# Modulation products moved into the branch tails of the first block, with the layer loop written out and one weight queue

## What is computed

```
def ada_mod(cvec, w, b):                       # w: 1024 x 6144, per layer
    return jnp.split(jax.nn.silu(cvec) @ w + b, 6, axis=-1)
...
x = first_block(...)
return second_block(x, c_2, ctx_2, c_ctx_2, ada_w_2, ada_b_2, ...)
...
# in second_block, for each of 2 layers:
sh1, sc1, g1, sh2, sc2, g2 = [... for m in ada_mod(c, ada_w[i], ada_b[i])]
csh1, csc1, cg1, csh2, csc2, cg2 = ada_mod(c_ctx, ada_w[i], ada_b[i])
...
# in first_block, the end of branch n:
sigmoid(merge[:, :, n]) * ((o * silu(gates[:, :, n])) @ w_branch[l, n])
```

## Time and profile before

| | |
|---|---|
| median of 3 runs | 5255.11 us (5243.96 to 5256.96) |
| the profiled execution | 5240.5 us, its span 5238.4 us |
| PE (TensorE matmuls) busy | 4346.1 us, 83% |
| PE weight loads busy | 3690.2 us, 70% |
| DVE (VectorE) busy | 1823.1 us, 35% |
| ACT (ScalarE) busy | 1476.7 us, 28% |
| POOL (GpSimd) busy | 1377.6 us, 26% |
| mean granted TensorE clock | 0.887 |

### The profile page before, as it was taken

How to read it: one execution, slowest core, us unless ns; L and a number is a source line. 1 busy time by engine, 2 the same in 40 slices (tenths; PEclk the granted TensorE clock), 3 DMA queues, 4 the chain that set the end, 5 groups by cost and what they waited for, 6 DMA issues and landing times. The chain is left out here.

```text
span 5238.4 us, 60561 instructions
## 1 busy us (share of the span) xinstructions
PE 4346.1 (83%) x24260; PEld 3690.2 (70%) x24260; DVE 1823.1 (35%) x3628; ACT 1476.7 (28%) x2338; POOL 1377.6 (26%) x468
## 2 busy tenths in 40 slices
PE   5798978788688988778687959999998888857888
PEld 4677867677576876767435958888887878746776
DVE  2724352423462434324002036311112655553111
ACT  2234232222233333223101136321112443432211
POOL 1121313223213222232000222122222545432333
PEclk7798989889779989889897979999998888778999
DMA  2111212211212122232363211122212011101232
GB/s 68 42 50 33 85 35 85 83 57 57 60 35 70 53 61 61 63 92 71 97 220 110 65 51 20 33 57 60 58 55 58 27 34 33 37 17 49 74 87 73
DMA packets 512868, 323.86 MB, mean 62 GB/s; under 512 B 60239, under 2 KB 508871, under 8 KB 512583
## 3 DMA queue, kind: packets, MB, share of 16 engines
q1 hardware_dynamic: 512582, 319.91, 21.2%
HBM read 316.13 MB, written 2.16 MB: 61 GB/s over the span
## 5 line engine op out<-in xcount | busy, mean ns | idle before, releaser
L70 POOL TENSOR_TENSOR w_lo<-w_raw,w_hi 128x2048 fp32r<-128x2048 f32 (+5 forms) x284 | 1126.5, 3967 | 3464.2 <-ACT w_hi L190 3464.2
L190 ACT ACTIVATE w_hi<-w_raw 128x2048 fp32r<-128x2048 f32 (+5 forms) x284 | 473.6, 1667 | 1724.3 <-PE psum L232 1683.4
L230 PE MATMUL psum<-xF_hi,w_hi 128*128 128x512 f32 x1232 | 488.4, 396 | 61.0 <-PEq L107 58.4
L231 PE MATMUL psum<-xF_lo,w_hi 128*128 128x512 f32 x1232 | 484.7, 393 | 0.0
L232 PE MATMUL psum<-xF_hi,w_lo 128*128 128x512 f32 x1232 | 484.2, 393 | 0.0
L230 PE MATMUL psum<-ffn_h_hi,w_hi 128*128 128x512 f32 (+1 forms) x1056 | 381.2, 361 | 43.5 <-POOL w_lo L70 21.3
L232 PE MATMUL psum<-ffn_h_hi,w_lo 128*128 128x512 f32 (+1 forms) x1056 | 377.9, 358 | 0.0
L231 PE MATMUL psum<-ffn_h_lo,w_hi 128*128 128x512 f32 (+1 forms) x1056 | 376.6, 357 | 0.0
L230 PE MATMUL psum<-w_hi,xF_hi 128*128 128x256 f32 (+2 forms) x960 | 283.3, 295 | 40.9 <-PEq L107 30.2
L230 PEld LDWEIGHTS psum<-xF_hi,w_hi 128*128 128x128 f32 x1232 | 234.8, 191 | 114.4 <-issue 61.7
L231 PE MATMUL psum<-w_lo,xF_hi 128*128 128x256 f32 (+2 forms) x960 | 282.4, 294 | 0.0
(11 more groups left out here) (502 smaller groups left out, 9216.2 us busy)
## 6 DMA issues: line engine op xcount, KB each, us to landing
w_raw<-in_w_in_dram SPq DMA_DIRECT2D x54, 1024.0 KB, 5.3
w_raw<-in_ada_w_dram SPq DMA_DIRECT2D x48, 1024.0 KB, 5.2
w_raw<-in_ffn_w_in_dram SPq DMA_DIRECT2D x88, 512.0 KB, 5.1
w_raw<-in_w_in_dram SPq DMA_DIRECT2D x82, 512.0 KB, 4.1
w_raw<-in_ffn_w_out_dram SPq DMA_DIRECT2D x32, 704.0 KB, 4.6
w_raw<-in_w_branch_dram SPq DMA_DIRECT2D x80, 256.0 KB, 4.3
w_raw<-in_hg_w_in_dram SPq DMA_DIRECT2D x40, 512.0 KB, 4.0
w_raw<-in_na_w_qkv_dram SPq DMA_DIRECT2D x12, 1024.0 KB, 5.1
```

Of the source, the lines that this page charges most:

```text
L70: return eng.tensor_tensor(pair.lo, src, pair.hi.bitcast(F32), ALU.subtract)
L190: act.activation(self.w(j).hi, self.raw_w(j), ACT.Copy).then_inc(self.high_done, 1)
L230: pe.matmul(out, left.hi, right.hi, start=first, stop=False)
L231: pe.matmul(out, left.hi, right.lo, start=False, stop=False)
```

## The change

1. `ada_w` leaves the weight queue. In each branch tail ScalarE issues the DMA of one 1 MB block of it into a single buffer of its own; TensorE multiplies it after merge step 1 to 5, with the eight chunks spread over four groups of 32 columns (PSUM partitions 0, 32, 64, 96), 32 stationary columns each of which two are not zero. ScalarE copies all 128 partitions out, and after the next merge step two float32 matmuls against a constant 0/1 matrix `fours` add the four groups and turn the result. VectorE adds the bias. Four tails of a layer take 5 blocks, the last one 4: 24 blocks for each of 2 layers.
2. Merge steps go round three pairs of banks, since banks 6 and 7 are taken.
3. The small columns and the sigmoid (`conditioning`) go to the start of the kernel, before the rotation tables. There the 18 gathers stand before the weight loads.
4. The loop over layers is written out, with one weight queue for the whole kernel; `layer_params` runs once, for both layers, with 12 DMAs. Flushes at the loop's end and before the second block are gone; `room` flushes where many semaphores are in use.

```diff
+    def room(self, n):
+        if len(self.spent) + n > 110:
+            self.flush(keep=(self.mm, self.high_done, self.low_done, *self.landed))
...
-def branch_tail(C, n, o, mixed):
+def branch_tail(C, w, l, n, o, mixed, mod):
...
+    blocks = range(5 * n, min(5 * n + 5, 24))
+    NM = len(blocks)
...
+                def modulate(i):
+                    if i == 0:
+                        pe.wait_ge(gated, 4)
+                    else:
+                        pe.wait_ge(ada_copied, i)
+                    pe.wait_ge(ada_in, 16 * (i + 1))
+                    for k in range(KD):
+                        r = slice(32 * (k % 4), 32 * (k % 4) + 32)
+                        last = pe.matmul(C.bank(6)[r, 0:256], mod.cc[:, k, :], ada_w[:, k, :], start=(k < 4), stop=(k >= 4))
+                    last.then_inc(ada_product, 1)
+
+                def turn_modulation(i):
+                    pe.wait_ge(ada_copied, i + 1)
+                    if i:
+                        pe.wait_ge(ada_added, i)
+                    for b in range(2):
+                        last = pe.matmul(C.bank(7)[:, 2 * b:2 * b + 2], ada_rows[:, i % 2, P * b:P * b + P], C.fours,
+                                         start=True, stop=True)
+                    last.then_inc(ada_turned, 1)
+
                 for fb in range(8):
-                    A, B = C.bank(2 * (fb % 4)), C.bank(2 * (fb % 4) + 1)
+                    A, B = C.bank(2 * (fb % 3)), C.bank(2 * (fb % 3) + 1)
...
-                    elif fb < 4:
-                        pe.wait_ge(gated, 2 * (fb - 2) + 2)
+                    elif fb == 2:
+                        pe.wait_ge(gated, 2)
                     else:
-                        pe.wait_ge(mixed_done, fb - 3)
+                        pe.wait_ge(mixed_done, fb - 2)
...
+                    if 1 <= fb <= NM:
+                        modulate(fb - 1)
+                    if 2 <= fb <= NM + 1:
+                        turn_modulation(fb - 2)
...
             @block.scalar
             def _(act):
+                def load_modulation(i):
+                    if i:
+                        act.wait_ge(ada_product, i)
+                    act.dma_start(ada_w[:, :, :], cols(w["ada_w_2"], l, 256 * blocks[i], 256)).then_inc(ada_in, 16)
+
+                load_modulation(0)
                 C.high_parts(act, base)
...
+                    if 1 <= fb <= NM:
+                        i = fb - 1
+                        act.wait_ge(ada_product, i + 1)
+                        if i + 1 < NM:
+                            load_modulation(i + 1)
+                        if i >= 2:
+                            act.wait_ge(ada_turned, i - 1)
+                        act.activation(ada_rows[:, i % 2, :], C.bank(6)[:, 0:256],
+                                       ACT.Copy).then_inc(ada_copied, 1)
...
+                    if 3 <= fb <= NM + 2:
+                        i = fb - 3
+                        dve.wait_ge(ada_turned, i + 1)
+                        at = C.bank(7)[:, 0:4].rearrange("p (b c) -> p b c", c=2)
+                        b = 2 * blocks[i]
+                        dve.tensor_tensor(mod.ada[:, l, b:b + 2, :], at, mod.bias[:, l, b:b + 2].unsqueeze(2).broadcast_to([P, 2, 2]),
+                                          ALU.add).then_inc(ada_added, 1)
...
-        C.flush()
...
-        with nc.Fori(0, 2) as l:
-            C.begin(first_layer_jobs(w, l))
-            layer_params(C, l, w)
+        layer_params(C, w, par, neg_lam, sub_gain)
+        for l in range(2):
...
-            C.flush()
...
-    jobs = []
-    for l in range(2):
-        jobs += in_pieces(of("ada_w_2", l, True), 0, 6 * D)
-    jobs += in_pieces(of("na_w_qkv_2", 0), 0, 3 * D) + in_pieces(of("na_w_o_2", 0), 0, D) + ffn_jobs(0)
+    jobs = in_pieces(of("na_w_qkv_2", 0), 0, 3 * D) + in_pieces(of("na_w_o_2", 0), 0, D) + ffn_jobs(0)
...
+            @block.sync
+            def _(sp):
+                for dst, src in loads:
+                    column_gather(sp, dst, src, columns_in)
+                C.start_weights(sp)
+                sp.wait_ge(columns_in, 16 * len(loads))
...
+def modulation_scales(C, mod, small):
...
+    with C.stage("chain") as (block, chain):
+        C.weights(block)
...
+        small = small_columns(C, ctx)
+        early = ctx.enter_context(ExitStack())
+        mod = Modulation(C, ctx, early)
+        C.begin(first_layer_jobs(w, 0) + first_layer_jobs(w, 1) + second_jobs(w))
+        conditioning(C, w, mod, small)
+        first_block(C, w, lat, hF[:, :, SEQ:768], mod)
```

More of the change, by code:

```diff
@@ L886, in branch_tail @@
         gg = ctx.enter_context(C.nc.sbuf_tensor(f"gg_{C.serial}", [P, 2, SEQ], F32))
-        with C.stage("turned", "o_ready", "gate_sig", "gated", "high", "low", "merge_sig", "mixed_done", "chain") as (
-                block, turned, o_ready, gate_sig, gated, high, low, merge_sig, mixed_done, chain):
+        with C.stage("turned", "o_ready", "gate_sig", "gated", "high", "low", "merge_sig", "mixed_done", "chain",
+                     "ada_in", "ada_product", "ada_copied", "ada_turned", "ada_added") as (
+                block, turned, o_ready, gate_sig, gated, high, low, merge_sig, mixed_done, chain,
+                ada_in, ada_product, ada_copied, ada_turned, ada_added):
             C.weights(block)
@@ L1672, in second_jobs, with __init__, sb, conditioning @@
     return jobs + in_pieces(of("hg_w_o_2", 0), 0, D) + ffn_jobs(1)
-def modulation(C, w, ada, small):
+class Modulation:
+    def __init__(self, C, ctx, early):
+        def sb(n, shape, ctx=early):
+            return ctx.enter_context(C.nc.sbuf_tensor(n, shape, F32))
+        self.ada = sb("ada", [P, 2, 48, 2], ctx)
+        self.cc = sb("cc", [P, KD, 32])
+        self.bias = sb("ada_bias", [P, 2, 48])
+def conditioning(C, w, mod, small):
     nc = C.nc
@@ L1694, in modulation @@
                      (small["hg_norm"], w["hg_norm_g_2"].rearrange("a p -> p a"))]
-            loads += [(bias[:, l, :], w["ada_b_2"][l:l + 1].rearrange("a (k p) -> p (a k)", p=P)) for l in range(2)]
+            loads += [(mod.bias[:, l, :], w["ada_b_2"][l:l + 1].rearrange("a (k p) -> p (a k)", p=P)) for l in range(2)]
             for name in ("norm1_g_2", "norm2_g_2"):
@@ L1705, in _ @@
                 C.low_parts(pool)
-            @block.sync
-            def _(sp):
-                C.start_weights(sp)
-                for dst, src in loads:
-                    column_gather(sp, dst, src, columns_in)
-                sp.wait_ge(columns_in, 16 * len(loads))
             @block.scalar
@@ L1779, in modulation, with _ @@
-        with C.stage("chain") as (block, chain):
-            @block.vector
-            def _(dve):
-                step = Chain(dve, chain)
-                for l in range(2):
-                    for q, name in ((1, "norm1_g_2"), (4, "norm2_g_2")):
-                        sc = ada[:, l, 8 * q:8 * q + 8, :]
-                        step(dve.scalar_tensor_tensor(sc, sc, 1.0, small[name][:, l, :].unsqueeze(2).broadcast_to([P, KD, 2]),
-                                                      ALU.add, ALU.mult))
+def modulation_scales(C, mod, small):
+    with C.stage("chain") as (block, chain):
+        C.weights(block)
+        @block.scalar
+        def _(act):
+            C.high_parts(act)
+        @block.vector
+        def _(dve):
+            step = Chain(dve, chain)
+            for l in range(2):
+                for q, name in ((1, "norm1_g_2"), (4, "norm2_g_2")):
+                    sc = mod.ada[:, l, 8 * q:8 * q + 8, :]
+                    step(dve.scalar_tensor_tensor(sc, sc, 1.0, small[name][:, l, :].unsqueeze(2).broadcast_to([P, KD, 2]),
+                                                  ALU.add, ALU.mult))
@@ L2490, in consts_table @@
     t["columns"] = np.concatenate(variants, 1)
+    t["fours"] = np.stack([p % 32 == c for c in range(2)], 1).astype(np.float64)
     t["inv_freq"] = np.broadcast_to(inv, (P, 24))
```

178 lines of the change are left out of this document (78 added, 100 removed).

## The result

The changed kernel is slower: 5359.62 us in the median (5345.36 to 5364.31) against 5249.53 (5240.03 to 5256.96) for the kernel before beside it, a ratio of 1.0208 (in brackets, here and below, its 95% interval: [1.0188, 1.0228]). The forecast was 5065 us. The head of the second block and the gap between the layers are gone but for a few us, as forecast; some 300 us came in that the sum did not have. The profiled execution took 5355.97 us, its span is 5354.0.

The account below looks back on a forecast made before the run. TensorE was taken to bound layers and tails; the second block's head and the layer gap were exposed. Terms -269 + 31 - 8 - 24 + 79 + 5 = -186 from 5240.5 gave 5054.5; with run spread, forecast 5065 us, range 5035 to 5180.

Parts of the forecast that it names:

- step 5: Waits and queues of the branch tails: ScalarE's wait and VectorE's addition cost nothing; late loads add 5 us (0 to 20).
- The prediction's own sign of being wrong: Wrong if the branch tails grow by more than 100 us or the start by more than 45.
- The second claim that failed: Stages from 2812 us on: the same instructions in both kernels, so no term in the sum.
- Step 1: Head of the second block, 274.3 us: all but 1.6 us and a 3.3 us later end goes, 269 us removed.
- Step 2: Conditioning at the kernel's start: gathers 14.5 us, then weights and low parts 16.5 us, 31 us added (26 to 41).
- Step 3: `layer_params` run once: 8 us removed in layer 1 (12.7 us left), 24 us in the gap before layer 2.
- Step 4: 48 modulation blocks in the tails: product 1.2 us and turn 0.44 us each, 79 us added (62 to 187).
- the figure for three tiles: Trainium skill's 2.38x for three column tiles: eight matmuls in a tail cost at least 1.45 us, sum 12 us higher.
- The rival of groups that take turns: Column groups in the tails do not overlap: 8 matmuls cost 3.46 us, 108 us more, 5173 us; chance 0.11.
- That of an emptying array: In the tails, each change between wide and narrow matmuls loses 0.163 us: 16 us, 5081 us; chance 0.12.
- Late loads: Modulation blocks landing late in a few places in the tails: 5 us added (0 to 20).
- The rival that made the kernel slower: Blocks land so late that 38 waits in the tails reach 4.9 us or more; at 6.2 us, 5300 us; chance 0.03.

Follow-up runs that it names:

- the first experiment: The changed kernel with VectorE's bias addition of a block put ahead of its wait for the merge step: 5087.94 us, ratio 0.9694.
- the change with 14 columns: The changed kernel with 14 unused columns added to the constants, nothing else changed: 5335.79 us, ratio 1.0185.

## Why the prediction was wrong, and where it was right

**The step that failed is step 5, its sentence on VectorE: "one operation on 4 columns for a block, beside 3.6 busy of 8.3 us; nothing".** It looked at how much VectorE had to do, not at what stood ahead of the addition in its queue, nor at who waited for it. For ScalarE's new wait the same step did name what was queued behind. For VectorE the question had to be asked the other way round: TensorE waits for `ada_added`, and the operation that raises it stands behind a merge-sum that depends on the TensorE step just finished. The price was in the rows of before. From the end of a merge step to the end of the sigmoid 544.70 to 546.67, 1.97 us; VectorE's merge-sum 3.58; the addition and the hand-over some 0.3, an estimate; less the 1.2 that the forecast gave to the product, which runs meanwhile: 4.65 us, 38 times 177. The trace of after says 4.83 in most steps and 179.3 in all. The rest, 87 us, is the lower clock, for which the earlier trace rows had a sign too: the gap between the layers, without TensorE, stood at 0.52. The prediction's own sign of being wrong, tails that grow by more than 100 us, came: 78 for the blocks and 268 for the waits.

**The second claim that failed** is that from 2812 us on both kernels do the same in the same time. The instructions are the same, the addresses of their activations are not. Putting these back on multiples of 64 bytes took 42 us of span off the first experiment and 25 off the change, over both blocks; of the 32 us by which the second block had grown, 24 and 21.5 went. The prediction looked for the price of each added operation and never asked what an added tensor moves.

**The other terms.**
- Step 1, head of the second block: 269 us forecast, 274.3 - 4.4 = 270 measured. Right, GpSimd's last low part included (4.50 us).
- Step 2, the conditioning: 31 forecast, 56.77 - 19.82 = 37 measured. The gathers took 18.7 us to issue, not 14.5 (the two bias rows 4.67 where 4 had been taken, four of `norm_g` 5.52 where 0.65 each had been), and VectorE's chain ended last, behind the sigmoids, not GpSimd:

```profile
19.82 0.37 SPq L1706 DMA_DIRECT2D c_in<-in_c_dram  x1
...
22.50 4.67 SPq L1706 DMA_DIRECT2D ada_bias<-in_ada_b_dram  x2
27.22 5.52 SPq L1706 DMA_DIRECT2D columns<-in_norm_g_dram  x4
...
38.55 16.77 SPq L168 DMA_DIRECT2D w_raw<-in_w_in_dram  x4
...
45.97 8.95 POOL L70 TENSOR_TENSOR w_lo<-w_raw,w_hi 128x2048 fp32r<-128x2048 f32 x2 [45.53 <-ACT w_hi L195]
...
56.12 0.17 DVE L1808 TENSOR_SCALAR columns<-columns 128x16 f32<-128x16 f32 x1
56.77 0.37 SPq L1054 DMA_DIRECT2D pos_i<-in_positions_dram  x1
```

- Step 3: `layer_params` from 105.17 to 117.75, 12.6 us (12.7 forecast); the gap between the layers 3.1 us where 28.6 were, 25 removed (24 forecast).
- Step 4: the product 9.60 - 8.42 = 1.18 us a step (1.2 forecast), the turn 0.45 (0.44). The 1.45 us that the prediction called the least by the figure for three tiles was no lower bound for four. The rival of groups that take turns is out by the run with one group. That of an emptying array is not: 1.18 is the 0.86 of four rounds and 0.32 more, just its price of 2 x 0.163, and with one group the step shows 12.17 - 8.42 = 3.75, 0.29 over the 3.46 forecast for one group. The forecast had this cost inside its 1.2 us as "some for the change"; the rival put it on top a second time.
- Late loads: 5 us forecast, none. The block lands in the time of the earlier trace rows, on the other queue too:

```profile
ada_w<-in_ada_w_dram ACTq DMA_DIRECT2D x48, 1024.0 KB, 5.2
```

- The rival that made the kernel slower had the right form, 38 waits of 4.9 us in the tails, and the wrong cause: a late block. Its chance of 0.03 was the chance of that cause alone.

**Together**, in spans: 5052 forecast (5054.5 less 2.1 outside the span), + 266 for the wait and its clock, + 42 for the operands' places, + 6 for the conditioning, - 7 for late loads and the borders = 5359, against 5354.0. The 266 and the 42 are differences between runs, so the test of the forecast is the kernel without them: its sum is 5051, its profile has 5045.7. Some of that closeness is luck, for the second block of that kernel is still 8 us longer than before, so the rest is some 13 us shorter than the sum. The structure of the forecast stood; one wait and one side effect were missing.

## What to carry to other kernels

For each semaphore that the bottleneck engine waits on, find the instruction that raises it and read what stands ahead of it in its own queue; if anything there depends on what the bottleneck has just finished, the wait is a full round trip each time, however small the operation. Count a wait on TensorE with the slower matmuls behind it, here half as much again (87 us on 179). And when a kernel gains or loses a small tensor, compare the steps of untouched stages too: they may have moved.

## What the hardware showed that was not expected

- Float32 matmuls in four groups of 32 columns run fully side by side: 8 of them in 1.07 us against 3.64 in one group. The Trainium skill ("TensorEngine Tiling (Array Packing)", "Key Properties") says that a change of tiling mode drains TensorE. The steps here agree with it: some 0.3 us beyond the columns' own time for the two changes of each block, with four groups and with one, 15 us for the 48 blocks. No run takes the change of mode alone away, so this is the likeliest reading, not shown.
- In the change the clock was at 1.2 GHz after each 4.83 us of waiting, and the rest of the step took 2.2 to 3.0 us longer. After 1.99 us most steps still lost 1.6 us (13.6 where wait and step are 12.0), but one in the change with 14 columns lost nothing (11.96). How much a wait costs was not a matter of its length alone.
- Adding 38 x 20 matmuls whose results are thrown away made a kernel 57 us faster.
- Activations 32 bytes off a multiple of 64 made merge steps 8.42 instead of 8.28 us, and two kernels 0.5 and 0.7% slower; a further 64 bytes made no difference in total, though single stages moved by some 20 us, one up and one down.
